# Ten of the experts' second-matrix loads issued as three, of 112, 8 and 8 partitions

## The chip, the cores and the metric

One core of a Trainium2 chip runs the whole program in one launch. The metric is the time of an execution on the device in microseconds (us); the kernel before took 1636.16 us (median of three runs, 1635.2 to 1639.25).

## What is computed

Two transformer-like blocks over 256 tokens of 1024 fp32 features. The first has an attention and convolution mixer and then a mixture of 32 experts, of which each token takes 4. It is the experts that matter here:

```python
def expert_step(acc, params):
    w1, b1, w2, b2, gate_e = params
    u = xt @ w1 + b1                      # w1 is 1024 x 2048
    glu = jnp.minimum(u[:, ::2], SWIGLU_LIMIT)
    lin = jnp.clip(u[:, 1::2], -SWIGLU_LIMIT, SWIGLU_LIMIT)
    a = glu * jax.nn.sigmoid(SWIGLU_ALPHA * glu) * (lin + 1)
    out = a @ w2 + b2                     # w2 is 1024 x 1024
    return acc + gate_e[:, None] * out.astype(jnp.float32), None
```

All weights are fp32: 8 MB of w1 and 4 MB of w2 for each expert, 384 MB in all. The second block has two layers with mixers and dense feed-forward parts (1024 x 2816 and back), and a last norm.

## The kernel before

The program writes its instructions out for each engine by hand, with semaphores between them. Its stages are the modulation and the projections of the first block, attention, the router, the experts, then the second block.

**The ring.** All large weights go through one SBUF buffer, `ring`: 128 partitions, 16 units of 8 KB per partition. `ring_order` (the order of all loads) gives each load a unit, or two neighbouring ones for a wide load (`wide`): all of the experts' w1 loads and the w2 loads of experts 0 to 30. For each unit it counts in `uses` how often the unit's semaphore will have been raised by 16 when a load is complete, and it keeps in `prior` which load lay there before. So the experts use the ring as eight slots of 16 KB per partition.

**The loads.** SP issues every load of the ring in that order, from `fill` (L3126 to L3132): it waits until the steps that read the unit's former content are done (L3131), then issues one DMA (L3132), which raises the unit's semaphore `s_slot[s]` by 16 when it has landed. Readers wait for the count that `units` holds. A wide load takes 512 rows of w2 (or 256 of w1), 2048 KB that are contiguous in memory, and puts 16 KB of them into each of the 128 partitions (L3188 and L3189 for w2). Each expert has six wide loads: four of w1 and two of w2, which `w2_order` numbers 0 and 2. The order is w1 (e, 2), (e, 4), (e, 6), then w1 (e+1, 0), then w2 (e, 0) and (e, 2) (L3182 to L3191). Expert 31 has its w2 as four loads of 1024 KB.

**The experts on the engines.** Tokens of an expert are gathered into up to 64 slots (32 more in a second pass where an expert has more). PE multiplies them with w1 in L939 (`mlp1`) and with w2 in L957 (`mlp2`), 64 stationary columns against 512 moving ones each; L948 turns the activations, L964 (`back`) adds the result to the tokens through a selection matrix, and L1252 does so for the last expert. L989 and L1002 are the second pass. DVE and ACT compute the activation and the sums between them (L2018 to L2045, L2672 to L2737). The buffers of the biases are filled by loads that POOL issues in its helper `small` (L2994): b_mlp goes as four loads into 32 partitions each (L3076, `B1raw[32 * j:32 * j + 32, :]`), and two more loads into 32 partitions.

The first wide load of the experts is issued at 141 us, while the first block's output projection is still being computed.

Of the kernel before, what the change touches and what calls it, by code (L numbers as in the profile page):

```python
# [16 lines left out]
UNIT = 2048  # L17
# [97 lines left out]
def w2_order(e):  # L115

    return (0, 2, 1, 3) if e == NEXP - 1 else (0, 2)


def wide(name):  # L120

    return name[0] == "w1" or name[0] == "w2" and name[1] < NEXP - 1


def front_order():

    order = []
    for n in range(16):
        order.append(("in", n // 2, n % 2))
        if 2 <= n < 10:  # L130
            order.append(("ada", 1, n - 2))
    return order


def ring_order():

    order = [("ada", 0, k) for k in range(8)] + front_order()
    first = len(order)
    order += [("scale2", k) for k in range(4)] + [("out", kk) for kk in range(4)] + [("gate2", k) for k in range(4)]
    experts = len(order)  # L140
    order += [("w1", 0, 0)]
    for e in range(NEXP):
        order += [("w1", e, k) for k in (2, 4, 6)]
        if e + 1 < NEXP:
            order += [("w1", e + 1, 0)]
        order += [("w2", e, k) for k in w2_order(e)]
    post = len(order)
    order += [("abc", c) for c in AB] + [("abr", kk) for kk in range(2)] + [("dft",), ("fm",)]
    order += [("outab", kk) for kk in range(4)]
    for l in range(2):  # L150
        if l:
            order += [("pool",), ("pmap",)]
        order += [(w, l, j) for j in range(NFF // 2) for w in ("gate", "up")]
        order += [("down", l, kk) for kk in range(NFF // 2)]
    units, uses, prior, at = {}, [0] * NRING, [None] * NRING, 0
    slots = list(range(8))
    for n, name in enumerate(order):
        if n == first:
            assert at % 2 == 0
            slots, at = [(at + i) % 8 for i in range(8)] + list(range(8, NRING)), 0  # L160
        if n == experts:
            slots, at = [14, 15, 12, 13, 0, 1, 2, 3, 8, 9, 10, 11, 4, 5, 6, 7], 0
        if n == post:
            slots, at = [14, 15, 0, 1, 2, 3, 4, 5, 6], 0
        s = slots[at % len(slots)]
        at += 1
        uses[s] += 3 if name[0] == "in" and name[1] >= 6 else 1
        before = [prior[s]]
        prior[s] = name
        if wide(name):  # L170
            t = slots[at % len(slots)]
            at += 1
            assert s % 2 == 0 and t == s + 1
            before.append(prior[t])
            prior[t] = name
        units[name] = (s, 16 * uses[s], [b for b in dict.fromkeys(before) if b is not None])
    return units


def build(nc, I, out, counts, counting):  # L180
    with ExitStack() as ctx:
        def sem(name):
            return ctx.enter_context(nc.semaphore(name))
# [3 lines left out]
        ring = ctx.enter_context(nc.sbuf_tensor("ring", [128, NRING * UNIT], F32))  # L187
# [14 lines left out]
        s_slot = [sem(f"s_slot{i}") for i in range(NRING)]  # L202
        s_load = {n: sem(f"s_load_{n}") for n in LOADS}

        def done(name):

            if counting and name not in counts:
                return sig["pe_ada"].sem, 1
            key, n = counts[name]
            return sig[key].sem, n  # L210

        units = ring_order()

        def held(name):

            c = name[2] % 2 if wide(name) else 0
            return (name[0], name[1], name[2] - c) if c else name, c
# [299 lines left out]
        def emptied(name):  # L517

            kind = name[0]
            if kind in ("in", "out", "abc", "abr", "gate", "up", "down"):  # L520
                st, n = {
                    "in": lambda: ("in", 4 * name[1] + 2 * name[2] + 1),
                    "out": lambda: ("out", 2 * name[1] + 1),
                    "abc": lambda: ("ab", 2 * AB.index(name[1]) + 1),
                    "abr": lambda: ("ab", 9 + 2 * name[1]),
                    "gate": lambda: (f"ffn{name[1]}", 4 * name[2] + 1),
                    "up": lambda: (f"ffn{name[1]}", 4 * name[2] + 3),
                    "down": lambda: (f"ffn{name[1]}", 2 * NFF + 2 * name[2] + 1),
                }[kind]()
                return [(st, "lo", n)]  # L530
            if kind == "w1":
                return [("w1", name[1], name[2] + 1), ("w1b", name[1], (0, 1, 2, 2)[name[2] // 2])]
            if kind == "w2":
                return [("w2", name[1], name[2] + wide(name)), ("w2b", name[1])]
            if kind == "dft":
                return [("width", 3)]
            if kind == "outab" and name[1] == 2:
                return [("outab", 3)]
            return [name]
# [15 lines left out]
        def _(pe):  # L555
# [52 lines left out]
            def project(*pieces):  # L608
                for n in pieces:
                    b, kp, w = n // 4, n % 4, IN_WIDE[n // 4]  # L610
                    _, hi, lo, _, _ = piece("in", n)
                    pe.wait_ge(*done(("in", "lo", n)))
                    if n == 4:
                        pe.wait_ge(*done("cwb"))
                    if b == 0:
                        pe.wait_ge(*done(("hTL", kp)))
                    for t in range(2):
                        if kp == 0 and 2 * b + t >= 3:
                            pe.wait_ge(*done(("land", (2 * b + t - 3) // 2, (2 * b + t - 3) % 2)))
                        for c in range(2):  # L620
                            k = 2 * kp + c
                            i = mm3(pe, PS[:, (2 * b + t) % 3, 0:w], hTH[:, k, t * 128:(t + 1) * 128],
                                    hTL[:, k, t * 128:(t + 1) * 128], hi[:, c, :], lo[:, c, :], k == 0, k == 7)
                        if kp == 3 and t == 0:
                            i.then_inc(*P.tick(("in", "first", b)))
                    i.then_inc(*P.tick(("in", "used", n)))
# [180 lines left out]
            def out_tile(k, i, ns):  # L807
                _, hi, lo, _, _ = piece("out", k)
                c = slice(512 * ns, 512 * ns + 512)
                return mm3(pe, PS[:, 2 * i + ns, :], yH[:, k, i * 128:(i + 1) * 128], yL[:, k, i * 128:(i + 1) * 128],  # L810
                           hi[:, c], lo[:, c], k == 0, k == 7)
# [2312 lines left out]

        @block.sync
        def _(sp):  # L3126
            def fill(name, view, src):
                s, _, before = units[name]
                for prior in before:
                    for step in emptied(prior):  # L3130
                        sp.wait_ge(*done(step))  # L3131
                sp.dma_start(view(ring[:, s * UNIT:(s + 1 + wide(name)) * UNIT]), src).then_inc(s_slot[s], 16)  # L3132

            def fill_rows(name, w, r0, nk, c0, ncol):
                fill(name, lambda u: u[:, 0:nk * ncol].rearrange("p (c n) -> p c n", c=nk),
                     w[r0:r0 + 128 * nk, c0:c0 + ncol].rearrange("(c p) n -> p c n", p=128))
# [40 lines left out]
            def w1(e, ks):  # L3177
                for k in ks:
                    fill(("w1", e, k), lambda u: u, w1_rows(e, k))

            w1(0, (0,))
            for e in range(NEXP):  # L3182
                w1(e, (2, 4, 6))
                if e + 1 < NEXP:
                    w1(e + 1, (0,))
                for k in w2_order(e):
                    if wide(("w2", e, k)):
                        fill(("w2", e, k), lambda u: u,  # L3188
                             I["w_mlp2"][0, e][k * 256:k * 256 + 512, :].rearrange("(p q) n -> p (q n)", q=4))  # L3189
                    else:  # L3190
                        fill_rows(("w2", e, k), I["w_mlp2"][0, e], k * 256, 2, 0, 1024)  # L3191

            with sp.If(sp.value_load(most, min_val=0, max_val=256) > LIMIT):
                for e in range(NEXP):
                    with sp.If(sp.value_load(cnt[0:1, e:e + 1], min_val=0, max_val=256) > LIMIT):
# [3 lines left out]
                        for k in range(4):  # L3199
                            u = ring[:, (8 + k) * UNIT:(9 + k) * UNIT].rearrange("p (c n) -> p c n", c=2)  # L3200
# [62 lines left out]
```

## Time and profile before

| what | value |
|---|---|
| median of three runs | 1636.16 us (1635.2 to 1639.25) |
| profiled execution, its own time | 1638.55 us |
| its span, first to last instruction | 1636.7 us |
| PE busy (matmuls) | 1528.5 us, 93% |
| DVE, ACT busy | 668.1 us, 454.1 us |
| moved by DMA | 534.25 MB, mean 326 GB/s |

The span is what the trace covers; the execution's own time has 1.85 us around it. In the slices of the page each digit is the busy share of a fortieth of the span, 40.9 us, in tenths. The DMA share is that of the 16 DMA engines together; the trace does not tell one of them from another.

### The profile page before, as it was taken

Reading aid. Unit: us, or ns where it says so; the run is one execution under the profiler, and the core shown is the slowest. Engines: PE = TensorE matmul, PEld = TensorE weight load, DVE = VectorE, ACT = ScalarE, POOL = GpSimd, SP = SyncE. Lnnn points to the kernel's source line nnn. Section 1 sums busy time; section 2 is a strip of 40 time slices with the busy share of each in tenths; the row PEclk is TensorE's granted clock in tenths of the full one; section 3 lists DMA queues with packets and bytes.
Section 4 is the critical chain, followed back from the end, with each engine's and each line's share of the span. In section 5 each row is a group of like instructions: output and inputs, shape, how many; then the busy total and the mean of one; then the engine's idle time right before and its main releaser. Section 6 shows DMA issues by size and latency. Waiting matters only on the chain. (4 is left out here: it accounts for less than half of the span.)

```text
span 1636.7 us, 21528 instructions
## 1 busy us (share of the span) xinstructions
PE 1528.5 (93%) x8591; PEld 868.7 (53%) x8591; DVE 668.1 (41%) x958; ACT 454.1 (28%) x754; POOL 107.3 (7%) x119
## 2 busy tenths in 40 slices
PE   6999999999999998999988989887999999999998
PEld 3888633333333333333332323222858998789986
DVE  3576632232222222233222222223866565465654
ACT  3475411111111111011110101002765444354443
POOL 4032200000000000000000000000530002200000
PEclk8999999999999999999999999999999999999999
DMA  9977799999999999999999999999536655466520
GB/s 366 336 223 271 311 378 426 425 420 414 426 425 426 426 427 426 426 426 426 425 425 426 427 423 426 427 424 336 183 103 219 186 190 190 129 208 191 181 103 26
DMA packets 109696, 534.25 MB, mean 326 GB/s; under 512 B 6770, under 2 KB 69897, under 8 KB 83041
## 3 DMA queue, kind: packets, MB, share of 16 engines
q1 hardware_dynamic: 107600, 529.97, 81.5%
q8 instruction: 121, 1.98, 0.5%
q0 software_dynamic: 1936, 1.98, 0.4%
q14 instruction: 39, 0.31, 0.1%
HBM read 530.87 MB, written 1.05 MB: 325 GB/s over the span
## 5 line engine op out<-in xcount | busy, mean ns | idle before, releaser
L939 PE MATMUL ps<-ring,arena 128*64 128x512 f32 x2040 | 490.9, 606 | 25.7 <-DMA ring<-in_w_mlp 23.8
L939 PEld LDWEIGHTS ps<-ring,arena 128*64 128x64 f32 x2040 | 130.6, 137 | 264.2 <-issue 211.7
L957 PE MATMUL ps<-ring,arena 128*64 128x512 f32 x1024 | 230.1, 598 | 13.8 <-DMA ring<-in_w_mlp 7.3
L1556 DVE TENSOR_TENSOR wl<-ring,wh 128x1024 fp32r<-128x1024 f32 x132 | 162.1, 1232 | 134.2 <-ACT wh L2427 134.2
L542 PE MATMUL ps<-hth,wh 128*128 128x256 f32 x704 | 200.1, 284 | 1.4 <-DVE htl L2218 1.4
L543 PE MATMUL ps<-htl,wh 128*128 128x256 f32 x704 | 197.8, 281 | 0.0
L544 PE MATMUL ps<-hth,wl 128*128 128x256 f32 x704 | 197.3, 280 | 0.0
L2018 DVE TENSOR_TENSOR arena<-ps,arena 128x1024 f32<-128x1024 f32 x68 | 83.3, 1224 | 262.3 <-PE ps L964 255.5
L2427 ACT ACTIVATE wh<-ring 128x1024 fp32r<-128x1024 f32 x132 | 139.3, 1060 | 147.1 <-PE ps L544 147.1
L957 PEld LDWEIGHTS ps<-ring,arena 128*64 128x64 f32 x1024 | 74.9, 137 | 162.0 <-issue 142.6
L2043 DVE TENSOR_TENSOR arena<-ps,arena 128x512 f32<-128x512 f32 x34 | 23.5, 691 | 330.2 <-PE ps L957 327.0
L543 PEld LDWEIGHTS ps<-htl,wh 128*128 128x128 f32 x704 | 134.7, 191 | 0.0
L542 PEld LDWEIGHTS ps<-hth,wh 128*128 128x128 f32 x704 | 132.5, 188 | 2.1 <-issue 1.0
L544 PEld LDWEIGHTS ps<-hth,wl 128*128 128x128 f32 x704 | 133.6, 190 | 0.0
L2691 ACT ACTIVATE arena<-arena 128x512 f32<-128x512 f32 (+1 forms) x33 | 20.4, 617 | 311.6 <-DVE arena L2031 311.6
L2712 ACT ACTIVATE obh<-arena 128x512 fp32r<-128x512 f32 x30 | 18.9, 630 | 286.8 <-DVE arena L2043 286.8
L542 PE MATMUL ps<-wh,fth 128*128 128x512 f32 x176 | 69.8, 396 | 0.0
L543 PE MATMUL ps<-wl,fth 128*128 128x512 f32 x176 | 69.6, 395 | 0.0
L544 PE MATMUL ps<-wh,ftl 128*128 128x512 f32 x176 | 69.5, 395 | 0.0
L2672 ACT ACTIVATE arena<-ps,arena 128x256 f32<-128x256 f32 x60 | 30.6, 560 | 120.2 <-PE ps L910 115.2
L3099 POOL MEMSET arena<- 128x1144 f32 x1 | 1.1, 1063 | 955.7 <-DVE htl L2218 955.7
L542 PE MATMUL ps<-wp,ht 128*128 128x384 f32 (+1 forms) x128 | 46.0, 360 | 1.5 <-DVE wp L1556 1.4
(446 smaller groups left out, 1845.8 us busy)
## 6 DMA issues: line engine op xcount, KB each, us to landing
ring<-in_w_mlp SPq DMA_DIRECT2D x190, 2048.0 KB, 29.5
ring<-in_w_ada SPq DMA_DIRECT2D x24, 1024.0 KB, 10.9
ring<-in_ffn_w_gate SPq DMA_DIRECT2D x22, 1024.0 KB, 5.4
ring<-in_ffn_w_up SPq DMA_DIRECT2D x22, 1024.0 KB, 5.4
ring<-in_ffn_w_down SPq DMA_DIRECT2D x22, 1024.0 KB, 4.8
ring<-in_w_in SPq DMA_DIRECT2D x10, 768.0 KB, 12.1
ring<-in_w_in_ab SPq DMA_DIRECT2D x6, 1024.0 KB, 11.5
ring<-in_w_out SPq DMA_DIRECT2D x4, 1024.0 KB, 5.0
```

The costliest lines, as they stand in the source:

```text
L542: pe.matmul(o, lh, rh, start=first, stop=False)
L543: pe.matmul(o, lh, rl, start=False, stop=False)
L544: return pe.matmul(o, ll, rh, start=False, stop=last)
L939: t = pe.matmul(PS[64 * g:64 * g + 64, HB[hb][ns], :], x[:, k8, :], u[:, f:f + 512], start=False, stop=k8 == 7)
L957: t = pe.matmul(PS[64 * g:64 * g + 64, 3, :], a4[:, kc, 64 * kg:64 * kg + 64], u[:, c, g * 512:(g + 1) * 512], start=k8 == 0, stop=k8 == 7)
L1556: dve.tensor_tensor(l, src, h.bitcast(F32), ALU.subtract).then_inc(*V.tick((st, "lo", n)))
L2018: dve.tensor_tensor(x, PS[:, b:b + 2, :], x, ALU.add).then_inc(*tick(name))
L2043: dve.tensor_tensor(OBF, PS[:, bank, :], G2R, ALU.mult).then_inc(*tick(n_f))
L2427: act.activation(h, src, ACT.Copy).then_inc(*S.tick((st, "hi", n)))
L2672: act.activation(XGT[b % 2][:, k, :], PS[:, bank, (k % 2) * 256:(k % 2) * 256 + 256], ACT.Identity, scale=a2[:, k:k + 1], bias=sh2[:, k:k ...
L2691: act.activation(SIG[:, 0:n], GLU[:, 0:n], ACT.Sigmoid, scale=1.702).then_inc(*Q.tick(name))
L2712: act.activation(OBH[0], OBF, ACT.Copy).then_inc(*SM.same())
```

## The change

A new function `uneven` picks ten loads: the w2 loads numbered 0 of experts 3, 6, 9, ..., 30. For these `fill` issues three DMAs in place of one, for partitions 0 to 111, 112 to 119 and 120 to 127 of the same buffer, from the same rows of the same matrix. Each raises the slot's semaphore by 16, and `ring_order` counts three for them, so that readers wait for all. What is waited for ahead of the first DMA is as before, and nothing is waited for between the three. All other loads keep their single DMA.

```diff
+def uneven(name):
+
+    return name[0] == "w2" and name[1] % 3 == 0 and name[1] and name[2] == 0
...
-        uses[s] += 3 if name[0] == "in" and name[1] >= 6 else 1
+        uses[s] += 3 if name[0] == "in" and name[1] >= 6 or uneven(name) else 1
...
-            def fill(name, view, src):
+            def fill(name, view, src, rows=((0, 128),)):
                 s, _, before = units[name]
                 for prior in before:
                     for step in emptied(prior):
                         sp.wait_ge(*done(step))
-                sp.dma_start(view(ring[:, s * UNIT:(s + 1 + wide(name)) * UNIT]), src).then_inc(s_slot[s], 16)
+                u = view(ring[:, s * UNIT:(s + 1 + wide(name)) * UNIT])
+                for p0, p1 in rows:
+                    sp.dma_start(u[p0:p1], src[p0:p1]).then_inc(s_slot[s], 16)
...
                         fill(("w2", e, k), lambda u: u,
-                             I["w_mlp2"][0, e][k * 256:k * 256 + 512, :].rearrange("(p q) n -> p (q n)", q=4))
+                             I["w_mlp2"][0, e][k * 256:k * 256 + 512, :].rearrange("(p q) n -> p (q n)", q=4),
+                             ((0, 112), (112, 120), (120, 128)) if uneven(("w2", e, k)) else ((0, 128),))
```

## Rows read from the trace of the kernel before

**Rows 1.** The page: busy tenths and rates in 40 slices.

```profile
PE   6999999999999998999988989887999999999998
DMA  9977799999999999999999999999536655466520
GB/s 366 336 223 271 311 378 426 425 420 414 426 425 426 426 427 426 426 426 426 425 425 426 427 423 426 427 424 336 183 103 219 186 190 190 129 208 191 181 103 26
```

**Rows 2.** Busy time by stretch; the last two columns are DMA share and GB/s.

```profile
core 0: us, PE busy (x) PEld busy (x) DVE busy (x) ACT busy (x) POOL busy (x), PEclk, DMA share, GB/s
337.00:390.00 53.00, 52.60 (x299) 17.22 (x297) 13.93 (x19) 6.35 (x13) 0.00 (x0) 1.00 0.99 411
...
390.00:1105.00 715.00, 663.49 (x3255) 229.90 (x3255) 185.98 (x249) 73.35 (x143) 0.00 (x0) 0.99 1.01 426
```

**Rows 3.** PE's waits in 390 to 1140 us, then its timeline and the chain there.

```profile
PE ps L939 <- DMA ring<-in_w_mlp: 23.8, 20, 2.9
...
PE ps L957 <- DMA ring<-in_w_mlp: 7.3, 7, 1.2
...
1120.61 2.92 PE L939 MATMUL ps<-ring,arena 128*64 128x512 f32 x8 [2.07 <-DMA ring<-in_w_mlp]
...
1138.27 0.97 PE ps L1252 x6
```

**Rows 4.** SP's waits, the DMA queues and loads in 390 to 1105 us.

```profile
SPq L3132 <- PE ps L939: 252.2, 70, 9.2
SPq L3132 <- PE ps L957: 156.9, 47, 5.8
SPq L3132 <- PE ps L927: 144.8, 24, 12.3
...
q8 instruction: 70, 1.15, 0.7%
...
ring<-in_w_mlp SPq DMA_DIRECT2D x144, 2048.0 KB, 32.8
```

**Rows 5.** The page: loads of the whole span, KB each, median us to landing.

```profile
ring<-in_w_mlp SPq DMA_DIRECT2D x190, 2048.0 KB, 29.5
```

**Rows 6.** Line 3132: duration of an issue in ns, min/median/max.

```profile
L3132 SPq DMA_DIRECT2D ring<-in_w_mlp x194: 327/328/8475, 141.1 to 1097.3; - x194
```

**Rows 7.** The last 25 us of the experts' loads, columns as in rows 2.

```profile
1105.00:1130.00 25.00, 18.64 (x78) 5.38 (x76) 6.98 (x12) 1.73 (x4) 0.00 (x0) 0.93 0.82 320
```

**Rows 8.** Loads of the biases, issued in 150 to 178 us.

```profile
arena<-in_b_mlp POOLq DMA_DIRECT2D x4, 128.0 KB, 11.3
arena<-in_b_mlp POOLq DMA_DIRECT2D x2, 64.0 KB, 6.8
```

**Rows 9.** Stretches with POOL's tiny loads, then those around the biases' loads.

```profile
6.00:12.00 6.00, 3.87 (x16) 0.43 (x16) 0.13 (x2) 0.00 (x0) 6.00 (x13) 1.00 1.03 410
12.00:20.00 8.00, 3.77 (x16) 0.40 (x16) 1.74 (x4) 3.95 (x7) 3.04 (x7) 1.00 0.99 368
150.00:155.00 5.00, 5.00 (x49) 1.98 (x42) 4.93 (x9) 1.05 (x2) 4.01 (x6) 1.00 1.04 436
157.00:170.00 13.00, 13.00 (x55) 10.09 (x54) 6.67 (x9) 6.37 (x10) 0.00 (x0) 1.00 1.01 344
170.00:175.00 5.00, 5.00 (x23) 4.14 (x23) 2.45 (x2) 1.77 (x2) 0.00 (x0) 1.00 1.02 433
178.00:184.00 6.00, 5.43 (x33) 4.64 (x32) 5.93 (x9) 2.01 (x6) 3.46 (x2) 1.00 1.01 378
```

## The prediction

> **What bounds the kernel now.** I read the slices of the page first. From the fifth slice to the twenty-seventh the DMA digit is 9 and the rate stays near 426 GB/s, while PE stands at 8 or 9 too [rows 1]. These are the experts. The table by stretches says which of the two is full: from 390 to 1105 us PE is busy 663.5 of 715 us, so it stands still for 51 us, and the DMA share is 1.01 throughout [rows 2]. The waits of PE in 390 to 1140 name the expert matrices' loads: 23.8 us before L939 and 7.3 us before L957 [rows 3]. SP, asked for its own waits in 390 to 1105, waits for PE to give buffers back (252, 157 and 145 us, its three largest sums), and yet a 2048 KB load lands 32.8 us after its issue [rows 4]: six to seven loads of 4.9 us (below) stand in the queue, so the engines that move data never run dry. From expert 7 or so on, then, the time is set by bytes over a full set of DMA engines. Before 390 it is not: in 337 to 390 PE is busy 52.6 of 53 us and the rate dips to 411 GB/s [rows 2]. The chain of waits is no help here, since of the experts it holds only the last step, L1252 at 1138.3 us [rows 3]; the page's chain goes on from there to the dense layers, which the change does not touch.
>
> How many loads lie where: 190 of 2048 KB in all and 144 of them issued from 390 to 1105 [rows 4, 5]. Expert e's first half of the second matrix is full-size load 6e + 6. So experts 3 and 6 (loads 24 and 42) fall among the first 46, before 390, and the eight of experts 9 to 30 fall where the DMA binds. One load at 426 GB/s is 2,097,152 B / 426 = 4.92 us; if 16 engines take 8 rows each, a row of 16 KB costs one engine 0.615 us.
>
> **The change part by part.**
> Issues: 20 more on SP. One takes 327 ns at the least [rows 6], so 6.5 us of SP in all. SP's waiting for PE, over 500 us, covers it, and behind each stand 30 us of queued loads. PE waits for 48 instead of 16 on the slot's semaphore, for the same bytes; the three are issued back to back with the buffer's waits ahead of the first alone, so no new wait holds up SP. I cost this at 0. Without the queue's depth it would be 0.65 us at each split load.
>
> Bytes and rows: unchanged. What moves is who carries them. 112 rows divide over 16 engines as 7 each; two sets of 8 rows can give at most eight engines one row each, twice. So in each split load eight engines take 9 rows and eight take 7: +0.615 us on the one half, -0.615 us on the other, 6.2 us over ten loads and 4.9 us over the eight that count. The Trainium skill, "DMA: Bandwidth & Descriptors", section "Why a DMA increments its semaphore by 16 and not by 1", names which: the count of engines is the largest up to 16 that divides the rows, and from SP it is the lowest-numbered ones; no row here names an engine.
>
> Is there an early half and a late one? The tail of the stage says so: from 1105 to 1130 us the rate is 320 GB/s and the DMA share 0.82 [rows 7], while PE still waits for a load at 1120.6 [rows 3]. Against 426 that is 106 x 25 = 2650 KB less, or 6.2 us of all engines: the mean engine is done 6.2 us before the last one. One cause is in the queue table: instruction loads, 70 of them and 0.7% of 16 engines' 715 us, which is 80 us of one engine [rows 4]; spread over half of the engines they are 10 us each. If the late half is the one relieved, up to 4.9 us is gained; if it is the one that takes the extra rows, 4.9 us is lost; if each half has late ones, little is won. I put 0 for this term and keep -4.9 and +4.9.
>
> Writing into 8 partitions: all loads of the ring write 128 partitions, so this operation is not in the trace. The nearest rows are the loads of b_mlp: four of 128 KB, each into 32 partitions, and then two of 64 KB [rows 8]. Around the first four the rate is 436 and 433 GB/s, and from 157 to 170 us it is 344 [rows 9]: 89 x 13 = 1157 KB missing, or 2.67 us for four loads, 0.67 us each, on top of their own bytes. From 178 to 184 us, with the other two, it is 378: 330 KB or 0.38 us each, half as much for half the bytes. That they come from POOL may be a part of it: POOL's many tiny loads run beside the weights at 410 GB/s from 6 to 12 us, but at 368 from 12 to 20 [rows 9]. An 8-partition load has the same 128 KB. Its bounds: 0 (0.615 us for a row as always, the eight engines side by side); and four times 0.67 = 2.67 us, since it hits a quarter of the partitions. I take twice, 1.33 us: b_mlp has 16 engines on 32 partitions, one for two, here 8 on 8, one for one. Two per split load, eight split loads: 16 x 1.33 = **21 us**. The 112-partition load reaches nearly all partitions as before; I put 0 for it, and its upper bound is the same 21% fall of the rate over its 4.3 us, some 1.1 us each or 9 us.
>
> Here the Trainium skill speaks against the change more strongly ("SBUF — State Buffer", section "Door 1: The DMA port swizzle"): groups of four neighbouring partitions share one of 16 ports, and a load into partitions 0 to 3 alone got 27.6 GB/s. By it 8 partitions are two ports, an estimate of 2.4 us per small load, and the sum would be 16 x 2.4 = 38 us instead of 21. By that rule the trace agrees that few partitions cost rate; how steeply, its row doesn't show.
>
> Sum: 0 (issues) + 0 (balance) + 21 (small loads) = +21 on the profiled execution's 1638.55 us, whose span is 1636.7; that execution lies 2.4 us over the median of 1636.16, so **1657 us** beside the median.
>
> **The rivals.** A difference of 0.3%, 4.9 us, is about what a measurement of this kernel can tell from none.
> 1. The small loads cost no more than their rows, and the balance brings little: 1636, between 1631.3 and 1641. For it: every 2048 KB load already runs back to back, and 128 KB is a sixteenth of one. And part of the dip may be POOL's way of issuing. Against it: the depth of the dip at 157 to 170. Chance 0.29.
> 2. Faster: the same, with all the late engines in the relieved half. Place: the last landing of expert 31. Price: -0.615 us for each of eight loads, or of ten if the first two count, bounded by the 6.2 us of the tail: 1631. It decides only if the two small loads together cost under 0.6 us more than their rows and the other half's latest engine was at least 9.8 us (twice 4.9) ahead. Chance 0.11.
> 3. Pile-up in full: eight engines with rows for the same 8 partitions queue behind one another, and behind the loads that write these anyway. Price 2.67 us each, 16 x 2.67 = 43: 1679, and with the 112-partition load's 9 us 1688. For it: the quarter of the partitions. Against it: engines that are 6 us early on average can absorb part. The Trainium skill's port rule named above is this mechanism. Chance 0.20.
> 4. The extra rows fall on the late half, and nothing else: +4.9, 1641. Chance 0.03.
> 5. It doesn't spread at all: if 8 rows go over one engine, that one gets 16 rows more and one less, 9.2 us per split load, eight times: 1710. Chance 0.03.
>
> **How the numbers follow.** The forecast has 0.34; rivals 3, 4 and 5 are slower too: 0.60 slower. Rival 1 is the 0.29 within 0.3%, rival 2 the 0.11 faster. The likeliest single case is 1657, its own range 1645 (half the price) to 1668 (plus the 112-partition term and 2). The range runs from 1631, rival 2, to 1700, which holds rival 3 with its extra and leaves out rival 5 and whatever is steeper.
>
> **What would show it.** Right: in 390 to 1105 of the new profile the rate falls below 426 once per three experts, with stretches of 2 us near 300 to 380 around each split load's landing; PE's waits for the expert matrices grow from 31 us by about 20; L1252 moves from 1138 to about 1159; everything after it keeps its length. The price is wrong if no such dips are there and the waits stay at 31. The balance term shows in the tail: if the late half was relieved, the last 25 us before expert 31's landings lie nearer to 426 than 320 GB/s. SP's issues should keep 327 ns at the least, and loads still land some 30 us after issue. The forecast is wrong at its root if PE's waits for loads grow and the total doesn't, for then the DMA was not the bound.

## The result and the profile after

The changed kernel takes 1780.84 us (median of 4 runs, 1772.0 to 1784.16) beside 1637.7 us for the kernel before (4 runs, 1635.2 to 1641.95): a ratio of 1.0858, interval 1.0839 to 1.0878, or 143 us more. The forecast was 1657, its range ended at 1700: the sign was right, the size was wrong by a factor of seven (21 against 143). The profiled execution took 1784.16 us with a span of 1782.3, 145.6 more than the span before.

The page of the changed kernel (lines below the change are numbered 5 higher: L944, L962 and L1257 are L939, L957 and L1252 of before). First busy tenths, clock and rates by slice, 44.6 us each, then the two costliest groups on PE and the loads:

```profile
PE   6999999999788788987768787786799999989998
PEclk9999999999999899999989899998999999999999
DMA  9968799999999999999999999999544655546530
GB/s 369 309 205 344 292 413 347 427 348 426 359 393 406 334 425 298 427 302 396 373 304 427 259 406 351 386 411 315 198 155 133 221 182 187 188 154 190 188 119 24
...
L944 PE MATMUL ps<-ring,arena 128*64 128x512 f32 x2040 | 508.6, 626 | 81.7 <-DMA ring<-in_w_mlp 79.3
...
L962 PE MATMUL ps<-ring,arena 128*64 128x512 f32 x1024 | 248.2, 634 | 61.5 <-DMA ring<-in_w_mlp 58.1
...
ring<-in_w_mlp SPq DMA_DIRECT2D x180, 2048.0 KB, 35.4
...
ring<-in_w_mlp SPq DMA_DIRECT2D x10, 1792.0 KB
```

Read the DMA row and the GB/s row together. Before, both were flat through the experts' stage [rows 1]. Now the busy share still is (9 in every slice up to the end of the stage), but the rate goes down and up, 348, 426, 359, 393. The busy share alone shows nothing at all of where 143 us went. PE, in turn, shows the starving: from the eleventh slice on mostly tenths of 6 to 8, where it had 8 or 9.

The same is sharper in stretches around the first split load (expert 3), columns as in rows 2. After:

```profile
277.00:283.00 6.00, 5.46 (x28) 2.07 (x28) 0.78 (x2) 0.60 (x1) 0.00 (x0) 1.00 0.99 421
283.00:300.00 17.00, 16.96 (x111) 6.67 (x107) 3.16 (x5) 1.85 (x4) 0.00 (x0) 1.00 1.01 223
300.00:305.00 5.00, 4.71 (x22) 1.27 (x18) 3.77 (x5) 0.63 (x1) 0.00 (x0) 1.00 1.00 419
...
390.00:1250.00 860.00, 705.99 (x3255) 232.87 (x3251) 186.03 (x249) 73.77 (x145) 0.00 (x0) 0.94 1.00 366
...
1283.00:1783.00 500.00, 477.45 (x3143) 426.35 (x3141) 300.36 (x407) 252.24 (x388) 55.06 (x43) 0.98 0.50 162
```

And the kernel before, in the same stretch and in the 499 us after its experts:

```profile
283.00:300.00 17.00, 16.93 (x109) 6.70 (x107) 3.33 (x6) 1.85 (x4) 0.00 (x0) 1.00 1.01 426
...
1138.00:1637.00 499.00, 475.94 (x3149) 424.37 (x3149) 300.89 (x408) 253.45 (x389) 55.32 (x43) 0.99 0.49 162
```

For 17 us the rate is 223 in place of 426 GB/s, 52% of it, at a DMA share of 1.01 both times: all engines busy, each byte taking twice as long. That is 203 x 17 = 3451 KB not moved, 8.1 us of the queue, for one split load of 2048 KB, and the slow stretch is far longer than the 4.92 us that the load's bytes take, so that its neighbours in the queue are slow as well. Over 390 to 1250 us the mean rate is 366: 60 x 860 = 51600 KB or 121 us missing, of which the tail that was there before [rows 7] is 6.2. That leaves some 115 us for the eight split loads of experts 9 to 30 and the end of expert 6's.

The holes are not all alike. After, for the split loads of experts 9 and 24, and then the last 25 us up to PE's last wait for an expert's load:

```profile
477.00:498.00 21.00, 12.13 (x43) 3.63 (x42) 4.44 (x6) 1.23 (x2) 0.00 (x0) 0.84 1.00 218
...
985.00:1022.00 37.00, 25.03 (x89) 7.87 (x89) 3.91 (x6) 2.44 (x5) 0.00 (x0) 0.82 1.01 239
...
1240.77:1265.77 25.00, 17.95 (x81) 5.35 (x81) 2.72 (x4) 1.23 (x2) 0.00 (x0) 1.00 0.41 153
```

Before, the 25 us up to the same wait, and the stretch that holds the first two of the loads:

```profile
1095.61:1120.61 25.00, 18.70 (x86) 5.49 (x83) 3.96 (x5) 1.23 (x2) 0.00 (x0) 1.00 0.93 381
...
240.00:390.00 150.00, 145.68 (x779) 50.88 (x777) 43.77 (x62) 16.80 (x33) 0.00 (x0) 1.00 1.00 421
```

Added up from the rates of single microseconds, the ten holes of the changed kernel miss 8.2, 8.2, 10.4, 11.9, 13.4, 16.2, 18.3, 19.0, 11.2 and 11.9 us of the queue, 129 us in all. The last 25 us miss (426 - 153) x 25 / 426 = 16.0 us where they missed 2.6 before. Together that is some 141 of the 143.7 us (about 1 us stands in both and is counted once). So all ten split loads count, not eight, the holes grow up to expert 24 (why the last two are smaller is open), and the tail is a part of its own.

PE's waits for the experts' loads in 390 to 1290 us, in us, times and the longest:

```profile
PE ps L944 <- DMA ring<-in_w_mlp: 79.3, 41, 5.7
PE ps L962 <- DMA ring<-in_w_mlp: 58.1, 26, 7.1
```

They were 23.8 and 7.3 [rows 3]: 106 us more. PE's busy time also grew, from 1528.5 to 1573.3 us over the span, 45 us, with the mean matmul of these two groups at 626 and 634 ns where it was 606 and 598, while the granted clock fell from 0.99 to 0.94 in the stretch [rows 2]. One such fall, after a pause of PE:

```profile
1208.00:1212.00 4.00, 0.00 (x0) 0.00 (x0) 0.00 (x0) 0.00 (x0) 0.00 (x0) 0.86 0.90 221
1212.00:1218.00 6.00, 5.86 (x16) 1.76 (x18) 0.00 (x0) 0.00 (x0) 0.00 (x0) 0.52 1.02 418
```

PE ran nothing for 4 us, and over the next 6 us the granted clock was 0.52, close to the lower of its two levels (1.2 of 2.4 GHz). Over the whole span PE's idle time rose by 100.8 us (108.2 to 209.0) and its busy time by 44.8, together the 145.6 us of the spans. Missing bytes on the one side, PE waiting or slow on the other: they are one loss seen twice, not two to be added.

The chain of work, in which the last step of the experts stood at 1138.27 [rows 3], now has

```profile
1281.95 0.97 PE ps L1257 x6
```

143.7 us later. The loss is in the experts' stage; what follows takes 500 us as it took 499.

### The profile page after: what moved, and what is told of

It reads as the page before. It is cut to its first block and busy times, and to the rows that moved or that the text cites. A ratio compares the mean times of both kernels' runs of the same rounds, so it can differ in the third digit from the quotient of the medians.

```text
span 1782.3 us, 21548 instructions
## 1 busy us (share of the span) xinstructions
PE 1573.3 (88%) x8591; PEld 875.9 (49%) x8591; DVE 667.7 (37%) x958; ACT 454.2 (25%) x754; POOL 107.2 (6%) x119
## 5 line engine op out<-in xcount | busy, mean ns | idle before, releaser
L944 PE MATMUL ps<-ring,arena 128*64 128x512 f32 x2040 | 508.6, 626 | 81.7 <-DMA ring<-in_w_mlp 79.3
L962 PE MATMUL ps<-ring,arena 128*64 128x512 f32 x1024 | 248.2, 634 | 61.5 <-DMA ring<-in_w_mlp 58.1
L944 PEld LDWEIGHTS ps<-ring,arena 128*64 128x64 f32 x2040 | 132.2, 141 | 335.5 <-issue 217.1
L962 PEld LDWEIGHTS ps<-ring,arena 128*64 128x64 f32 x1024 | 75.9, 145 | 228.1 <-issue 140.7
## 6 DMA issues: line engine op xcount, KB each, us to landing
ring<-in_w_mlp SPq DMA_DIRECT2D x180, 2048.0 KB, 35.4
```

The lines of the kernel that those rows point to most:

```text
L944: t = pe.matmul(PS[64 * g:64 * g + 64, HB[hb][ns], :], x[:, k8, :], u[:, f:f + 512], start=False, stop=k8 == 7)
L962: t = pe.matmul(PS[64 * g:64 * g + 64, 3, :], a4[:, kc, 64 * kg:64 * kg + 64], u[:, c, g * 512:(g + 1) * 512], start=k8 == 0, stop=k8 == 7)
```

## The experiments

Two theories stood against each other. One: a load costs by how many partitions it has, so the small loads are the price (my forecast, or the pile-up of rival 3). Two: it costs by which partitions its engines write, whatever their number. Others beside them were the mere number of loads, and rows unevenly spread over the engines. Each time is given beside the median of the kernel before in runs on the same chip. Unless something else is said, the ten loads of the change are the ones split.

**Other cuts of the same ten loads.** The rows of each, in place of (0, 112), (112, 120), (120, 128):

```
-  ((0, 112), (112, 120), (120, 128))
+  ((0, 112), (112, 128))          # 112 and 16
+  ((0, 96), (96, 128))            # 96 and 32
+  ((0, 64), (64, 128))            # 64 and 64
+  ((0, 120), (120, 128))          # 120 and 8
```

112 and 16:

> The ten split loads go out as two, of 112 and 16 partitions; both divide over 16 engines, so each engine again has 8 rows (7 and 1). Theory A, the 112-partition load is what costs: its 7 rows per engine no longer fall on the partitions that the same engine writes in a full load, so two engines at a time write to the same group of partitions and the rate halves: most of the 143 us stays, 1730 to 1785. Theory B, the two 8-partition loads cost (eight engines on a few partitions): they are gone, and 16 engines with one row each are left: 1636 to 1665. Theory C, the imbalance of 9 and 7 rows costs: gone, 1634 to 1640.

1773.33 us beside 1638.33, ratio 1.0823 [1.0797, 1.0848]. With the two 8-partition loads merged into one of 16, 135 of the 143 us remain. The rate where the first split load goes:

```profile
285.00:290.00 5.00, 5.00 (x28) 1.59 (x23) 1.38 (x2) 0.63 (x1) 0.00 (x0) 1.00 1.01 220
```

In the trace each of the two loads raises its semaphore 16 times, once for each engine that took part. So, dealt evenly, every engine has one row of the one and seven of the other: no imbalance in rows, and the time is almost as bad.

96 and 32:

> The ten split loads as two, of 96 and 32 partitions: 6 and 2 rows per engine, 8 in all as before. Theory A1, the engines take neighbouring rows and any count other than the full 128 puts two engines on one group of partitions: as slow as 112 and 16, 1730 to 1785. Theory A2, only the odd count of 7 rows per engine (112) is bad: 1636 to 1660.

1797.76 us beside 1638.95, ratio 1.097 [1.0901, 1.1038], slower still than the 1730 to 1785 of theory A1.

64 and 64:

> The ten split loads as two, of the lower and the upper 64 partitions: 4 rows per engine each. By the port rule 64 partitions reach half of the 16 ports, so each half takes as long as a full load now does, 4.9 us: +4.9 us in each of the eight to ten split loads that count, 1677 to 1687 (theory A1, with no after-effects). If such a load also slows its neighbours in the queue, as the 112-partition load seems to do at 13 us a piece, 1720 or more. Theory A2 (only 7 rows per engine is bad): 1636 to 1650.

1784.51 us beside 1638.95, ratio 1.0889 [1.0851, 1.0927].

```profile
283.00:298.00 15.00, 15.00 (x95) 5.81 (x92) 2.61 (x3) 1.85 (x4) 0.00 (x0) 1.00 1.01 240
```

120 and 8:

> The ten split loads as two, of 120 and 8 partitions. If 120 rows go over 15 engines with 8 rows each, the engines keep whole blocks of 8 rows, one engine has none, and eight engines take one row more. Theory A1 (anything but 128 misplaces rows): 1700 to 1785. Theory A2 (only 7 rows per engine): 1636 to 1650. The 8-partition load alone, as a term: under 10 us in all, since 112 and 16 came out within 11 us of 112, 8 and 8.

1766.14 us beside 1638.95, ratio 1.0777 [1.069, 1.0864].

Per split load these four are 13.5, 15.9, 14.6 and 12.7 us, and the change 14.3. Each of the four stands on two runs, up to 23 us apart, so their order is not shown. The slowest has no load under 32 partitions, and two halves of 64, which can divide evenly over sixteen engines, cost as much as 112, 8, 8. So neither small loads nor unevenly divided rows are needed for the loss.

**Is it the number of loads?** Columns instead of partitions:

```
+  SPLIT = [(slice(0, 128), slice(0, 3584)), (slice(0, 128), slice(3584, 4096))]
...
-  for p0, p1 in rows:
-      sp.dma_start(u[p0:p1], src[p0:p1]).then_inc(s_slot[s], 16)
+  for p, c in rows:
+      sp.dma_start(u[p, c], src[p, c]).then_inc(s_slot[s], 16)
```

> Control: the split load as two loads of all 128 partitions, of 14 KB and 2 KB per partition. All theories: no difference, 1634 to 1640. If splitting a load at all costs, a few us more.

1639.96 us beside 1638.33, ratio 1.0006 [0.9997, 1.0016]: no difference. The rate is that of before:

```profile
390.00:1105.00 715.00, 664.15 (x3260) 228.57 (x3258) 186.48 (x250) 74.55 (x146) 0.00 (x0) 0.99 1.01 426
```

And so are PE's waits for these loads, L947 standing for L939 [rows 3]:

```profile
PE ps L947 <- DMA ring<-in_w_mlp: 20.9, 19, 1.5
```

So one load as two of all 128 partitions is free, with 1792 and 256 KB, the bytes of the split 112 | 16.

**Small loads beside a full one.** 128 partitions of 3584 columns, and the last 512 columns by 16 loads of 8 partitions, neighbouring ones or 4 apart:

```
+  [(slice(0, 128), slice(0, 3584))] + [(slice(8 * i, 8 * i + 8), slice(3584, 4096)) for i in range(16)]
+  [(slice(0, 128), slice(0, 3584))] + [(slice(b + j, b + j + 29, 4), slice(3584, 4096))
+                                       for b in (0, 32, 64, 96) for j in range(4)]
```

Neighbouring:

> No 112-partition load: the split load is one of 128 partitions with 7/8 of the columns (14 KB per partition) and 16 loads of 8 neighbouring partitions with the last 2 KB each. Each of these 16 goes over eight engines, so the shares of the engines are 9 and 7 rows' worth as in the change, and the bytes that go through 8-partition loads are the same 256 KB per split load. Theory A (the 112-partition load): only the small loads' own price is left, 1640 to 1660. Theory B (8-partition loads pile up): about the change's time, 1720 to 1790. Theory C (imbalance): as the change, 1780.

1668.98 us beside 1638.33, ratio 1.0182 [1.0167, 1.0197], 9 us beyond the nearest of the three ranges.

4 apart:

> As the previous one, but the 16 small loads take 8 partitions that are 4 apart (0, 4, ..., 28 and so on), so that by the port rule no two of the eight engines write the same group. Theory A and theory B both: no pile-up, only the shift of one row's worth from eight engines to the other eight in ten loads, of which eight count: 1631 to 1641, and the sign tells whether the late half of the engines was relieved (minus) or loaded (plus). If the number of loads is what costs (17 per split load, 160 more in all), 1650 or more. Theory C (imbalance): 1780.

1665.3 us beside 1638.33, ratio 1.0163 [1.0147, 1.0179]. Theories A and B had both asked for 1631 to 1641 here and missed; only the guess on the number of loads (1650 or more) fits. 160 small loads of 16 KB cost 31 and 27 us, a fifth of the change's loss. Neighbouring or spread makes little difference, as again at expert 15 below, where it turns out that small loads into the upper partitions cost and such into the lower ones don't.

Five of the loads (every second), with 3072 columns and 16 spread ones of 1024:

> As e8_spread, but in five loads (experts 6, 12, 18, 24, 30), and with 4 KB per partition in the small loads: the same bytes are shifted to the eight engines (two rows' worth in five loads for one row's worth in ten), with 80 small loads instead of 160. If the 27 us of e8_spread are the price of the number of small loads: half, 1650 to 1654. If they are the price of the shifted bytes: 1660 to 1668.

1658.07 us beside 1641.03, ratio 1.0103 [1.0083, 1.0123]: 17 us. With half as many small loads, each twice as large, and the same bytes in all, the loss is between half of the 27 us (13.5) and the whole, and between the two ranges expected. A price by the load and a price by the byte both stay possible; it isn't settled.

**One load alone.** The change for one expert only, 15 or 30:

```
-    return name[0] == "w2" and name[1] % 3 == 0 and name[1] and name[2] == 0
+    return name == ("w2", 15, 0)      # or ("w2", 30, 0)
```

Expert 15:

> The change for one load only, that of expert 15 (112, 8 and 8 partitions). If each split load costs its own share of the 143 us, 14 us over ten or 18 over eight: 1648 to 1657. If the cost grows with the number of split loads that went before, because each leaves the engines further apart and the next then meets them so: under 8 us, 1639 to 1646.

1650.77 us beside 1638.95, ratio 1.0065 [1.0043, 1.0088], 11.8 us.

```profile
635.00:640.00 5.00, 4.91 (x27) 1.86 (x26) 1.22 (x1) 1.22 (x3) 0.00 (x0) 1.00 1.10 416
640.00:662.00 22.00, 18.32 (x141) 6.96 (x139) 6.77 (x14) 1.23 (x2) 0.00 (x0) 0.92 0.98 201
662.00:667.00 5.00, 4.05 (x20) 1.06 (x16) 0.00 (x0) 0.00 (x0) 0.00 (x0) 1.00 1.04 439
```

One hole in the rate, with sharp edges: (426 - 201) x 22 = 4950 KB, 11.6 us of the queue. That is the measured loss, so the hole accounts for all of it.

Expert 30, near the end of the stage, on the guess that the price grows as the engines drift apart (the hole was 17 us long at expert 3 and 22 at expert 15):

> The change for expert 30 alone (112, 8 and 8 partitions). Theory P with the spread of the engines: early engines write misplaced rows into groups at which late ones still work on the loads before, so the slow stretch lasts as long as the engines are apart plus the load itself. At expert 15 it was some 20 us at about 195 GB/s, +12 us in all; at expert 30 the engines are furthest apart: +15 to +22, 1652 to 1660. If each split load has a fixed price: +12, 1648 to 1652.

1653.4 us beside 1641.03, ratio 1.0079 [1.0058, 1.0099], 12.4 us:

```profile
1078.00:1098.00 20.00, 12.14 (x44) 3.18 (x40) 2.61 (x3) 0.83 (x2) 0.00 (x0) 0.83 1.01 274
...
1100.00:1114.00 14.00, 8.20 (x38) 2.77 (x38) 3.95 (x5) 1.23 (x2) 0.00 (x0) 0.98 0.99 245
```

The hole is longer and shallower, (152 x 20 + 181 x 14) / 426 = 13.1 us, and the loss hardly more than at expert 15. The time lies in the range of the growing price (1652 to 1660), but only because the kernel before took 1641 there: the difference of 12.4 us is that of the fixed price. So for a load that is split alone the place matters little. Among the ten it is otherwise: expert 15's hole, 11.6 us alone, is 13.4 there, and the holes go on to 19.0 (expert 30's, though, is 13.1 alone and 11.9 among the ten). Ten at 12 us would be 120, not 143; the larger holes and the longer tail are the rest.

The trace shows how far the engines are apart, since each of the 16 raises of a slot's semaphore has its time. In the kernel before, the first and the last raise of one load are 1 us apart at 143 us, 4.2 at 283, 6.9 at 638 and 15.8 at 1045: the lengths of the holes that have no split load ahead of them (17 us at expert 3, the first of ten, 22 at 15 alone, some 36 at 30 alone) grow with it. In the changed kernel, of the load that starts to land at 1189.9 us, thirteen raises come within 2 us, two more after 12 and 14 us, and the last after 36. PE waits for that last one.

**Expert 15's load as 16 small ones,** without a large one beside them: 8 partitions each with their full 16 KB, 4 apart or neighbouring.

```
+  [(slice(b + j, b + j + 29, 4), slice(0, 4096)) for b in (0, 32, 64, 96) for j in range(4)]
+  [(slice(8 * i, 8 * i + 8), slice(0, 4096)) for i in range(16)]
```

4 apart:

> One split load only (expert 15), as 16 loads of 8 partitions that are 4 apart, 16 KB per partition. Only eight engines carry it, 16 rows each in place of 8: 4.9 us more for these, none for the others. Theory P (ports: engines lose time when several write to the same group of partitions): the eight write to eight different groups, so little beyond this: 1639 to 1646. Theory Q (any load that isn't of 128 partitions disturbs the queue, wherever it writes): 12 us or more, as for 112, 8 and 8 at this place: 1650 or more.

1652.81 us beside 1641.03, ratio 1.0076 [1.0057, 1.0095]. The theory of ports had asked for 1639 to 1646, so as I had put it, it missed, and theory Q's 1650 or more came true. But the rate told more than the sum:

```profile
640.00:643.00 3.00, 2.97 (x43) 1.68 (x41) 1.10 (x3) 0.00 (x0) 0.00 (x0) 1.00 0.99 421
643.00:661.00 18.00, 14.85 (x106) 5.12 (x102) 6.22 (x13) 1.23 (x2) 0.00 (x0) 1.00 1.03 226
```

The hole starts 3 us later than in the run with 112, 8, 8 at expert 15, as if the first of the 16 loads, which write partitions 0 to 63, went at full rate and only the later ones, into 64 to 127, did not.

Neighbouring:

> The same load as 16 loads of 8 neighbouring partitions: the same engines, rows and number of loads, but eight engines on two groups of partitions at a time. Theory P: eight rows through two groups take 2.4 us at the rate of one engine per group, 16 times is 39 us instead of 10: 20 to 35 us above the previous kernel, 1660 to 1680. Theory Q: the same as the previous kernel, within 3 us.

1655.3 us beside 1641.03, ratio 1.0091 [1.0072, 1.0109]. Theory P had asked for 20 to 35 us above the spread ones and theory Q for the same within 3; the difference is 2.5 us. So this pair spoke for Q, and a price for how few groups of partitions a small load reaches is not borne out by it.

```profile
641.00:669.00 28.00, 18.54 (x147) 6.90 (x145) 7.99 (x15) 1.23 (x2) 0.00 (x0) 0.90 1.01 240
```

**The lower or the upper half.** Then only the destination was changed. Eight spread loads of 8 partitions each, the same rows of the source, once into partitions 0 to 63, once into 64 to 127. In both, the other half of the buffer keeps what was there, so half of the load's bytes are left out; in the high run the upper half gets the rows of the lower.

```
+  [(slice(b + j, b + j + 29, 4), slice(0, 4096)) for b in (0, 32) for j in range(4)]    # low
+  [(slice(b + j, b + j + 29, 4), slice(0, 4096)) for b in (64, 96) for j in range(4)]   # high
...
+  sp.dma_start(u[p, c], src[slice(p.start - 64, p.stop - 64, p.step), c])                # high
```

Low:

> One split load only (expert 15), and only its lower half is loaded (partitions 0 to 63; 64 to 127 keep what was there): eight loads of 8 partitions that are 4 apart, so that each of the eight engines would write just the groups of four partitions that it writes in a full load. Theory P (two engines on one group of partitions halve each other): nobody meets anybody, the rate stays at 400 or more, 1634 to 1642. Theory S (a load of fewer than 128 partitions halves the rate of all wherever it writes): a stretch of some 10 us near 213 GB/s, 1642 to 1648.

1638.35 us beside 1638.71, ratio 1.0001 [0.9988, 1.0013].

```profile
639.00:660.00 21.00, 19.66 (x155) 7.57 (x153) 7.73 (x15) 1.23 (x2) 0.00 (x0) 1.00 1.01 427
```

High:

> As g1_low, with the same number of loads and the same source rows, but into partitions 64 to 127 (0 to 63 keep what was there). Theory P: the same eight engines now write the groups of the other eight, which are at their full loads: two writers on each, a stretch of 10 to 20 us near 213 GB/s. Theory S: as g1_low, whatever that is.

1649.02 us beside 1638.71, ratio 1.0074 [1.0051, 1.0097].

```profile
639.00:660.00 21.00, 17.91 (x129) 6.96 (x127) 8.00 (x15) 1.61 (x4) 0.00 (x0) 0.92 1.01 227
```

This is the pair that decides. Number, size, stride, source rows and place in the queue are equal; the destination alone moved, and with it 427 GB/s became 227 for 21 us, at a DMA share of 1.01 in both. The hole is (426 - 227) x 21 / 426 = 9.8 us, the times differ by 10.7. Theory Q (S here) is out, since the low run's loads have as few partitions and kept 427 GB/s.

The raises in the trace add two things. Each of the eight small loads brings eight raises as its data land, so eight engines carry it. And the full load ahead of them in the queue is slowed too: its last raise comes at 655.6 us in the high run, at 645.7 in the low one and at 645.3 in the kernel before.

**Halves taken another way.** Even and odd partitions, 64 each, the whole load:

```
+  [(slice(0, 127, 2), slice(0, 4096)), (slice(1, 128, 2), slice(0, 4096))]
```

> The whole load for expert 15 as two, of the even and the odd partitions, 64 each, 4 rows per engine. All groups of partitions are in use at once, but engines take neighbouring rows of a load and so share them in pairs. Theory P: two writers on a group only part of the time: less than the 12 to 15 us of a split by halves, 1640 to 1650. Theory S: as a split by halves, 1652 to 1656.

1640.17 us beside 1638.71, ratio 1.0008 [0.9994, 1.0023], no difference that can be told; the partial price that theory P had put on it is not there:

```profile
639.00:660.00 21.00, 19.80 (x155) 7.57 (x153) 7.49 (x15) 1.23 (x2) 0.00 (x0) 1.00 1.00 424
```

Partitions 0 to 63 as one load, with the other half left out:

```
+  [(slice(0, 64), slice(0, 4096))]
```

> Expert 15's load as one of partitions 0 to 63 only (64 to 127 keep what was there), 4 rows per engine over 16 engines. Theory P: sixteen engines on eight groups, a stretch of 5 us at half the rate plus the time by which the engines are apart. Theory S: the same; this is for the size of the stretch next to g1_low, which writes the same partitions with eight engines.

1643.26 us beside 1638.71, ratio 1.0032 [1.0016, 1.0048]: 4.6 us slower although 1 MB less is loaded, which at 426 GB/s is 2.5 us. The rate from 639 to 660 us:

```profile
639.00:660.00 21.00, 19.26 (x153) 7.16 (x151) 6.82 (x15) 1.23 (x2) 0.00 (x0) 1.00 0.99 267
```

Its price is then about 7 us, and two such halves would be 14: the cut 64 | 64 has 14.6 per load. The same 64 partitions went in for nothing as eight spread loads (the low run). The partitions are the same, so it must be how they are dealt to the engines.

**Three loads that cost nothing.** All ten, as even partitions (64) and two sets of every fourth (32 each):

```
+  [(slice(0, 127, 2), slice(0, 4096)), (slice(1, 126, 4), slice(0, 4096)), (slice(3, 128, 4), slice(0, 4096))]
```

> The ten loads of the change as three each, as in the change, but of the even partitions (64), of 1, 5, 9, ... (32) and of 3, 7, 11, ... (32): 4, 2 and 2 rows per engine. Theory P (two engines on one group of partitions): as one load of the even and one of the odd partitions cost nothing, all ten together cost nothing either: 1634 to 1642. If three loads for one cost something by their number or because they have fewer than 128 partitions: 1650 or more.

1640.72 us beside 1638.61, ratio 1.0007 [0.9994, 1.0019]: the number of loads of the change, split by partitions as in the change, and no difference that can be measured, nor any hole where the change has its first, nor a lower rate later:

```profile
283.00:300.00 17.00, 16.94 (x109) 6.76 (x107) 3.16 (x5) 1.84 (x4) 0.00 (x0) 1.00 1.01 427
390.00:1105.00 715.00, 663.40 (x3261) 229.63 (x3261) 186.81 (x250) 74.56 (x146) 0.00 (x0) 0.99 1.01 426
```

No version came out faster than the kernel before.

## Why the prediction was wrong in size

What is shown: around each load that is cut into ranges of neighbouring partitions the whole queue, this load and the ones beside it, moves at about half its rate (201 to 240 in place of 426 GB/s) for 15 to 22 us, and up to 37 us late in the stage. For small loads the destination partitions alone decide it (427 against 227 GB/s with all else equal). And the engines of one load finish up to 16 us apart in the kernel before and up to 36 in the changed one. What is argued from it: in a load of 128 partitions each engine writes partitions that no other engine writes, so full loads can follow one another at different speeds on different engines and never meet. A load of 112 neighbours divides its rows at other places, so that most engines write where others, on the loads before or behind, are writing, and two on one place get half each; interleaved sets divide like the full load. No row names an engine, so this stays an inference. It fits the cuts by partitions, but not all that was expected from it came true: the neighbouring small loads cost only 2.5 us more than the spread ones, and even and odd partitions cost nothing where a part was expected. The Trainium skill's rule ("SBUF — State Buffer", section "Door 1: The DMA port swizzle") has partitions 0 to 63 on one half of the ports and 64 to 127 on the other, and "DMA: Bandwidth & Descriptors", section "Why a DMA increments its semaphore by 16 and not by 1", puts an 8-partition load on the eight lowest-numbered engines. The trace agrees on eight by its raises; it doesn't say which. Sections "The descriptor swizzle" and "Back-pressure in remote DMA" of the same page add that in a 128-partition load each engine has one port of its own, and, of transfers between cores, that a saturated port stalls the engines' other queues too, which would carry the loss from one port further. The low and the high run agree with the rules on engines and ports together, 1638.35 against 1649.02 us: by them the low eight engines write their own ports in the one, and those of the other eight in the other. No run here shows a single port.

By the steps of the prediction:

**What bounds the kernel: right, but from earlier on.** The DMA bound the experts' stage, and each us lost there moved the end: the hole of 11.6 us at expert 15 cost 11.8, L1257 came 143.7 us later for 143 of the median, and the rest of the span kept its length. Rate would not have been lost at so direct a price had PE been the bound. But "Before 390 it is not" was wrong. From 240 to 390 us the queue already ran at 421 GB/s and a share of 1.00, and the loss only adds up if the holes of experts 3 and 6 (8.2 us each) count too: ten loads, not eight. A small misreading did no harm: in rows 1 the DMA digit is 9 from the sixth slice on, not the fifth (7, 311 GB/s), and the rate is near 426 from the seventh.

**Issues, at 0: right.** Two or three whole issues in place of one cost nothing where the partitions fit (0.1%, within the measurement, in both runs). SP kept its 328 ns at the median in the changed kernel; the least was 287:

```profile
L3139 SPq DMA_DIRECT2D ring<-in_w_mlp x214: 287/328/1613, 141.6 to 1239.9; - x107
```

**Balance, at 0 with 4.9 us to either side: not the cause, and 0 was about right.** The cut 112 | 16 has, dealt evenly, seven rows and one for every engine, eight as in the full load, and lost 135 us. The low run tries the other side: eight engines have their eight rows, the other eight have none, and the rate stays whole. Of the next load (last raise at 655.5 us before), eight of the 16 raises then come some 4.9 us earlier, but three of the late ones stay, and the last is at 653.3: 2.2 us gained there, and nothing that can be told in the time (1638.35 against 1638.71). So each half has late engines, the case in which the prediction said that little is won, and rival 2's condition was not met, if the small loads of the change go over the same eight engines as those of the low run. Its sign in the tail came out the other way, 153 GB/s where a relieved late half was to bring more than 320, but as the holes push the engines apart, the tail of the changed kernel doesn't measure the balance: with 112 | 16, which has none, the last 25 us have 175.

**The small loads, 1.33 us each: not refuted, and beside the point.** Merging them into one of 16 partitions saved 8 us of 143, within what the runs scatter (1772 to 1784 against 1769 to 1777). Eight of them into the upper partitions cost 10.3 us, 1.29 each, eight into the lower ones nothing; a price by the number of partitions, which I drew from b_mlp's loads [rows 8, 9], is therefore no law, and its agreement is luck. By 1.29 each, the 20 small loads would be 26 of the 143 us, an estimate; no run has them in their own place without the 112-partition load.

**The failed step** is "The 112-partition load reaches nearly all partitions as before; I put 0 for it". By exclusion it holds the greatest part of the loss: 135 us remain when both small loads are gone, and 64 | 64, without any load so small, loses 146. No run has the 112-partition load without its rest. I asked how many partitions the load reaches, which is nearly all; I should have asked whether each engine still writes the partitions that it writes in every other load, which after a cut at 112, by the inference above, hardly any does. Its upper bound was wrong in the same way: 21% off its own 4.3 us, 1.1 us. Even half the rate over its own bytes alone would have been 4.3 us; what was measured is half the rate over 22 us at expert 15 and 11.8 us lost by the one load: the loads around it were slowed with it. A second step made the miss larger, the one that counted each split load by itself: the holes grew from 8 to 19 us as the engines came apart. Pricing by own bytes is also why even rival 3, which had the mechanism (engines behind one another on the same partitions, and behind the full loads), ended at 1688: it priced the meeting for the small loads alone. The Trainium skill's port rule, an estimate of +38 us as I had applied it, pointed the right way, since the two runs on the halves fit it; but I used it as a price for few ports, which the neighbouring small loads at expert 15 don't bear out, and held it against only two of the three loads.

**What would show it.** Dips of 2 us to 300 to 380 GB/s were expected; there were holes of 17, 21 and 37 us at 223, 218 and 239 (experts 3, 9 and 24). PE's waits were to grow by 20 and grew by 106. Loads were to land some 30 us after issue and took 35.4. That everything after the experts keeps its length held.

## What to carry to other kernels

Before a load is cut by partitions in a queue that is the bound, look at which engine will write which partitions, not at how many partitions a load has: ranges of neighbours (64 | 64 as much as 112 | 8 | 8) halved the rate of all loads around them, 12 to 16 us for each 2 MB cut, while a cut by columns, or one into even and odd partitions or every fourth, was free. Price an operation that the trace doesn't have by what it does to all the work in flight beside it, since its own bytes can be the smaller part: here 4.9 us of bytes and 8 to 19 us lost. And look at how far the engines are already apart, since up to expert 24 each split load cost more after others. And where a DMA-bound stage slows, read the rate beside the busy share.

## What was not expected of the hardware

- Half rate at full busy share: 223 GB/s at a share of 1.01, where 426 GB/s had the same 1.01.
- The slow stretch outlasts the load: 17 us at expert 3 and 22 us at expert 15 (split alone) for bytes of 4.92 us, and in the run into the upper partitions the load ahead in the queue lands 10 us later.
- The engines of one queue drift apart in a full stream of equal loads, from 1 us to 16 us between the first and the last engine of a load over 900 us; ten split loads made it 36, with one engine far behind the rest.
- Leaving out half of a load's bytes made the kernel slower, 1643.26 against 1638.71 us, where the half that was left had 64 neighbouring partitions.
- Even and odd partitions as two loads cost nothing (ratio 1.0008, interval 0.9994 to 1.0023), two halves of 64 neighbours 14.6 us a load, as the mean of ten.
- PE, kept waiting by loads, also computed slower: the mean 128x512 matmul took 626 and 634 ns instead of 606 and 598, at a granted clock of 0.94 in the stretch instead of 0.99. The missing bytes already account for the time, so this is no loss beside them.
